# Two-layer hybrid encoder trunk: in the attention loop ScalarE copies every turned probability block two steps behind, and a finished pair's output one step earlier

## The reference, cut to what matters

```python
def block_attention(q, k, v, scale, diag_mask, cum=None):
    for q0 in range(0, S, Q_BLOCK):                # 4 blocks of 128 queries
        q1 = q0 + Q_BLOCK
        s = einsum('bhqd,bhkd->bhqk', q[:, :, q0:q1], k[:, :, :q1]) * scale
        if cum is not None:                        # second attention (FoX)
            s = s + cum[:, :, q0:q1, None] - cum[:, :, None, :q1]
        ...                                        # causal mask
        p = softmax(s, axis=-1)
        outs.append(einsum('bhqk,bhkd->bhqd', p, v[:, :, :q1]))
...
o_a = block_attention(qa, ka, va, mla_scale, chunk_mask) @ w_bo_a
o_b = block_attention(qf, kf, vf, fox_scale, frame_mask, cum) @ w_bo_b
```

## Time and profile before

| | |
|---|---|
| median of 3 runs | 1770.97 us |
| profiled execution | 1771.1 us, its span 1769.3 us, granted TensorE clock 0.996 |
| TensorE busy | 1731.1 us (98%) |
| VectorE busy | 1092.0 us (62%) |
| ScalarE busy | 681.6 us (39%) |
| GpSimd busy | 206.6 us (12%) |

### The profile page before, as it was taken

How to read it: one execution, slowest core, us unless ns; L and a number is a source line. 1 busy time by engine, 2 the same in 40 slices (tenths; PEclk the granted TensorE clock), 3 DMA queues, 4 the chain that set the end, 5 groups by cost and what they waited for, 6 DMA issues and landing times.

```text
span 1769.3 us, 21975 instructions
## 1 busy us (share of the span) xinstructions
PE 1731.1 (98%) x7813; PEld 1375.2 (78%) x7813; DVE 1092.0 (62%) x1647; ACT 681.6 (39%) x1125; POOL 206.6 (12%) x145
## 2 busy tenths in 40 slices
PE   5999999999999999999999999999999999999998
PEld 4777777777888888888877777777778888888886
DVE  7688888757545555543348888867665555555222
ACT  4445544434343233322235555552433422233222
POOL 3621100010020000001125200000100200000010
PEclk9999999999999999999999999999999999999999
DMA  4432211323333333333333312114233333333231
GB/s 124 106 75 75 57 52 42 85 82 95 101 100 94 99 99 95 95 91 95 95 86 70 102 54 60 48 36 113 78 89 113 95 97 98 101 96 92 87 97 69
DMA packets 308468, 152.19 MB, mean 86 GB/s; under 512 B 30436, under 2 KB 307166, under 8 KB 308396
## 3 DMA queue, kind: packets, MB, share of 16 engines
q1 hardware_dynamic: 308096, 151.05, 30.4%
q10 hardware_dynamic: 300, 0.19, 0.0%
HBM read 149.09 MB, written 2.10 MB: 85 GB/s over the span
## 4 chain that ended last, share of the span: by engine, by line
PE 87%; DVE 8%; ACT 3%; issue 2%; DMA 0%; SPq 0%; ACTq 0%; DVEq 0%
PE bank L1293 65%; PE bank L1370 12%; PE bank L1351 4%; PE bank L1403 2%; PE bank L1382 2%; DVE w_lo L912 2%; ACT w_hi L622 1%; DVE h_lo L941 1%; DVE c_acc L972 0%; DMA x_rows<-in_x 0%; DVE tmp L933 0%; PE bank L1318 0%; PE bank L1511 0%; DVE c_raw L1122 0%; DVE rstd_kv L946 0%
## 5 line engine op out<-in xcount | busy, mean ns | idle before, releaser
L622 ACT CAST w_hi<-raw 128x1024 fp32r<-128x1024 f32 (+4 forms) x330 | 301.3, 916 | 733.4 <-PE bank L1293 732.2
L912 DVE TENSOR_TENSOR w_lo<-raw,w_hi 128x1024 fp32r<-128x1024 f32 (+4 forms) x330 | 355.6, 1080 | 239.1 <-ACT w_hi L622 237.8
L1293 PE MATMUL bank<-h_hi,w_hi 128*128 128x512 f32 (+1 forms) x1200 | 474.8, 396 | 10.4 <-DVE w_lo L912 5.4
L1293 PE MATMUL bank<-h_hi,w_lo 128*128 128x512 f32 (+1 forms) x1200 | 468.1, 390 | 0.0
L1293 PE MATMUL bank<-h_lo,w_hi 128*128 128x512 f32 (+1 forms) x1200 | 468.0, 390 | 0.0
L1293 PEld LDWEIGHTS bank<-h_hi,w_hi 128*128 128x128 f32 (+1 forms) x1200 | 225.1, 188 | 69.4 <-issue 12.2
L1293 PEld LDWEIGHTS bank<-h_lo,w_hi 128*128 128x128 f32 (+1 forms) x1200 | 225.2, 188 | 48.9 <-issue 2.5
L1293 PEld LDWEIGHTS bank<-h_hi,w_lo 128*128 128x128 f32 (+1 forms) x1200 | 225.1, 188 | 48.4
L933 DVE TENSOR_TENSOR tmp<-bank,rstd_x 128x512 f32<-128x512 f32 x140 | 96.6, 690 | 267.7 <-PE bank L1293 259.2
L972 DVE SCALAR_TENSOR_TENSOR c_acc<-u_pad,dwk_l,c_acc 128x512 f32<-128x512 f32 x240 | 178.6, 765 | 1.1
L511 POOL TENSOR_TENSOR x_acc<-x_acc,x_sq 128x512 f32<-128x512 f32 x39 | 66.8, 1713 | 881.9 <-ACT x_sq L632 549.2
(11 more groups left out here) (207 smaller groups left out, 2149.0 us busy)
## 6 DMA issues: line engine op xcount, KB each, us to landing
raw<-in_w_in SPq DMA_DIRECT2D x96, 512.0 KB, 3.7
raw<-in_w_ffn_gate SPq DMA_DIRECT2D x44, 512.0 KB, 3.7
raw<-in_w_ffn_up SPq DMA_DIRECT2D x44, 512.0 KB, 3.7
raw<-in_w_ffn_down SPq DMA_DIRECT2D x32, 512.0 KB, 3.7
raw<-in_w_out SPq DMA_DIRECT2D x16, 512.0 KB, 3.8
raw<-in_w_ffn_down SPq DMA_DIRECT2D x16, 384.0 KB, 3.3
raw<-in_w_bo_a SPq DMA_DIRECT2D x16, 256.0 KB, 2.7
raw<-in_w_bo_b SPq DMA_DIRECT2D x16, 256.0 KB, 2.7
```

Of the source, the lines that this page charges most:

```text
L622: last = nc.scalar.copy(to, of)
L912: last = nc.vector.tensor_tensor(to, of, part.bitcast(F32), ALU.subtract)
L1293: ins = nc.tensor.matmul(bank_t[0:rows, :], wt[slot][:, w], x, start=first and k == 0 and p == 0, stop=last and k == k_tiles - 1 and p == 2)
```

## The change

In ScalarE's list for the attention loop, the copy of a transposed block now stands two steps behind its step without exception: block s = 0 is copied in step s = 2, and `pair_out` of the pair before follows it there. Nothing is added or removed, and no other engine's list is touched. One line less is in the file, so what stood from line 672 on now stands one line higher (912 becomes 911).

```diff
                                          accum_out=row_sum[:, s % 4:s % 4 + 1]).then_inc(exp_done, 1)
-                    if s == 3 and pair:
-                        turn(g - 3)
+                    if g >= 2:
+                        turn(g - 2)
+                    if s == 2 and pair:
                         pair_out(pair - 1)
-                    if g >= 2 and (s != 2 or not pair):
-                        turn(g - 2)
                     if g - 2 in FEED_END:
                         split(QKV + FEED_END.index(g - 2) + 2)
                         evac.add()
```

## The result

The changed kernel takes 1781.9 us, the median of 4 runs (1780.75 to 1782.91), against 1771.03 us for the kernel before on the same chip (4 runs, 1770.85 to 1771.8). The ratio is 1.0062 with a 95% interval of 1.0048 to 1.0077: 10.9 us slower. The forecast was 1779.4 us, 8.4 us slower than its own base. The profiled execution took 1782.45 us, its span is 1780.6 us (before 1769.3).

A forecast was written before the change was run, and what follows sets the result against it. TensorE, busy 98%, was taken as the bound. The profiled 1771.1 us + 8.04 us of four waits + 0.4 us beside GpSimd gave 1779.5 us, 1779.4 us for the median; own range 1778 to 1781, wider range 1776 to 1784 us.

The forecast's parts named there:

- Where the kernel is bound: TensorE, busy 98% of the span, sets the time; ScalarE's 11.8 us of copy waits in the first attention loop cost nothing.
- The win of 0 us: Earlier copy and `pair_out` release nothing TensorE waits for; gain bounded by 0 and 0.6 us, taken as 0.
- The path through the cast: Pairs 2 and 5: late `w_hi` cast delays `w_lo` by 3.81 and 3.93 us, then taps, maximum, scaling, TensorE's transposes.
- Size of the four waits: TensorE waits 2.12 us at step 19 and 1.90 us at step 43, in both layers: 8.04 us.
- GpSimd beside `w_lo`: Pair 5: late `w_lo` meets GpSimd's `ob_lo`; bounds 0 to 0.53 us, taken as 0.2 us, 0.4 us in two layers.
- The other five pairs: Pairs 1, 3, 4, 6, 7: late exponential stays hidden, cost nothing; 0.6 us in all if pairs 1 and 4 doubled.
- What is late next: After step 19's wait: step 20's scaling, the late `w_lo` and its `raw` buffer are late, but none reaches TensorE.
- The rule weighed: VectorE's queue is strict first-in first-out; otherwise step 19's scaling would cost TensorE at most about 0.1 us.
- The clock falls in the waits: Rival: all four new TensorE waits bring a clock fall of 2.2 us each, 8.8 us added, 1788.3 us; chance 0.07.
- The granted clock stays where it was: Expected sign in the changed kernel's profile: no change of the granted clock.
- the prediction's own test: Wrong if the four waits are missing, time does not grow by their sum, or transposes wait in the other five pairs.
- The idle 1.83 us near the start: Evidence weighed for the clock rival: after this TensorE idle, at 16.95, no slow matmuls are seen.

The follow-up runs named there:

- experiment 1: Changed kernel, but in pairs 2 and 5 ScalarE casts `w_hi` ahead of the copy and `pair_out`, as before the change: 1771.04 us, ratio 1.0.
- Experiment 2: Kernel before, with only the `w_hi` cast of pairs 2 and 5 put behind `pair_out` in step s = 3: 1781.62 us, ratio 1.0057.
- Experiment 3: Changed kernel, but VectorE makes `w_lo` of pairs 2 and 5 one step later, behind the scaling of steps 19 and 43: 1773.12 us, ratio 1.0012.
- 5 to 7: Changed kernel with VectorE taps at steps 19 and 43 changed: one less 1777.82 us, two less 1776.19 us, one more 1785.33 us.
- change again: Changed kernel run and profiled once more, unedited: 1781.76 us, ratio 1.0059.
- experiment 4: Kernel before, with the change made in pair 2 of each layer alone: 1776.46 us, ratio 1.0032.

## Why the prediction was right, and where its size was off

- **Where the kernel is bound** was right. ScalarE's stall grew by 20 us in the first layer's loop. In experiment 1 it is 18 us longer than before, and the time is that of the kernel before. The win of 0 us was right too: experiment 1 has the earlier copy and `pair_out` and is at 1.0.
- **The path through the cast** was right in each link: copy, `pair_out`, cast, `w_lo` 3.7 us late, two taps, maximum, scaling. Experiment 2 makes it alone, 1 takes it away, 3 cuts it at `w_lo`, and 5 to 7 lengthen and shorten it by 0.66 us per tap.
- **Size of the four waits**: forecast 2 x (2.12 + 1.90), in fact 7.94 us. In pair 2 the wait is 1.93 us instead of 2.12. I measured from the weight load at 191.81, but its matmul starts 0.22 us later (192.03 before the change); behind the wait load and matmul both start at 193.81. The lead of the load is eaten by the wait. In pair 5 the same 0.2 us were offset by the next point. TensorE's matmul at step 19 before the change (its load is in the earlier trace rows):

```profile
192.03 0.60 PE L1382 MATMUL bank<-ident,p_b 128*128 128x128 f32 x4
```

- **GpSimd beside `w_lo`** was right in kind, 0.2 us forecast in both layers. The two rows in pair 5 of layer 0, changed kernel:

```profile
260.09 1.27 POOL L517 TENSOR_TENSOR ob_lo<-o_raw,ob_hi 128x512 fp32r<-128x512 f32 x1 [21.68 <-ACT ob_hi L660]
...
260.99 1.46 DVE L911 TENSOR_TENSOR w_lo<-raw,w_hi 128x1024 fp32r<-128x1024 f32 x1 [4.05 <-ACT w_hi L622]
```

  `w_lo` takes 1.46 instead of 1.22 us, 0.24 us more. In layer 1 it is the same:

```profile
1131.29 1.46 DVE L911 TENSOR_TENSOR w_lo<-raw,w_hi 128x1024 fp32r<-128x1024 f32 x1 [3.85 <-ACT w_hi L622]
```

  With the stretch and without the lead of the load, the forecast 1.90 us becomes 1.90 + 0.24 - 0.22 = 1.92 us. The wait in layer 1 is 1.94 us. In layer 0 it is 2.13 us, and the other 0.2 us lie in ScalarE's list of pair 5, where the first copy of `pair_out` starts 0.37 us after the copy of the block:

```profile
258.57 0.27 ACT L652 COPY p_t<-bank 128x128 f32<-128x128 f32 x1 [4.94 <-PE bank L1402]
258.94 0.59 ACT L659 COPY o_raw<-bank 128x512 f32<-128x512 f32 x1
```

  In layer 1 it is 0.16 us (1129.07 and 1129.23), as at this place before the change (256.74 and 256.90). What holds it up isn't shown. Waits and GpSimd together: 7.94 us, forecast 8.44.
- **The other five pairs** were right: no transpose waits there. VectorE waits 1.3 us at most for a late exponential, but where a cast follows it then waits less for that: in pair 1 of layer 0 1.31 us for the exponential and 0.53 instead of 1.25 us for the cast. `w_lo` starts at 169.45 (forecast: about 169.7), the scaling of step 12 ends at 172.07, and TensorE's load is at 172.65.
- **What is late next** was right for the changed kernel: nothing behind the four waits. Experiment 3 showed how thin that was: 1 us more for VectorE's taps ahead of step 22 came with 1.1 us of waits of TensorE.
- **The rule weighed**: the trace bears out the order of the list. VectorE idled 3.47 and 4.05 us with ready taps behind `w_lo` (pairs 2 and 5 of layer 0), and in experiment 3, with `w_lo` behind the scaling, the wait at step 19 shrank to 0.22 us.
- **The step that was mis-sized: the clock.** "The clock falls in the waits" was priced as none or all four, at 2.2 us each and a chance of 0.07. It happens to single waits. Of the 14 waits of 1.9 to 2.1 us in four profiled executions (change, change again, experiments 2 and 4) 8 were followed by half clock, 1.65 to 1.72 us each. In the profiled execution the two falls, 3.36 us, less the 0.50 us that the waits were smaller than forecast, are 2.9 of the 2.95 us between the sum (1779.5 us) and 1782.45 us. "The granted clock stays where it was" was therefore wrong. The mean of 0.996 hides it, because 7 us at half clock weigh little among 1780 and because the record of this trace misses the slow start.

  By the prediction's own test ("if they are there and the time does not grow by their sum") it failed here: the waits sum to 7.9 us, and the time grew by 10.9. The result lies outside the forecast's own range of 1778 to 1781 us. That it lies inside 1776 to 1784 us is in part luck, since the room there was meant for small stalls in the other pairs, which didn't come, and the falls filled it.

  My reasons were two. The idle 1.83 us near the start seemed to show that such a gap is free, and a dense stream around the waits seemed to protect. But the gap near the start can't show a fall at all. The transposes on both sides of it, in the kernel before:

```profile
11.44 3.67 PE L1442 MATMUL bank<-ident,x_rows 128*128 128x128 f32 x16 [1.65 <-DMA x_rows<-in_x]
16.95 1.85 PE L1442 MATMUL bank<-ident,x_rows 128*128 128x128 f32 x12 [1.83 <-DVE x_t L1059]
```

  Ahead of the gap they start 0.21 us apart, twice the 0.11 us of a transpose in the attention loop, so TensorE was still slow, with no full clock to fall from; behind the gap many are 0.11 us apart. And the stream around the four waits is as dense as anywhere, and the clock fell in it.

Not settled: what decides whether one wait of some 2 us brings a fall. The wait, the work around it and the kernel are the same in the two profiles of the change, so the instruction lists alone don't decide it.

## What to carry to other kernels

In an in-order list, ask of an instruction that will wait not only what it wins but what ready work stands behind it, and follow that work to the bound engine: here 1 us of cast behind a free stall became 2 us of TensorE idle, four times. Before paying for a stall removed, check that it is on the engine that sets the time. And price a new gap in a full TensorE stream at its length plus a possible stretch at half clock, with a spread, instead of as one number.

## What the runs showed of the hardware that was not expected

- After a wait of about 2 us in a stream that is otherwise 98% busy the granted clock fell from 2.4 to 1.2 GHz in 8 of 14 cases, and each fall cost 1.65 to 1.72 us. After 2.6 to 2.8 us it fell in 2 of 4, after 0.6 to 1.5 us in none of 8. The same wait brings a fall or doesn't from one execution to the next. Two falls more or less would make the 3.4 us of spread of the changed kernel's single executions (1780.75 to 1784.13 us), against 0.95 us before; falls themselves are seen only in the profiled executions.
- Of an overlapping GpSimd subtraction and a VectorE tap, the one that starts second is stretched by nearly the whole overlap: two taps from 1.41 to 2.40 us, or GpSimd's operation from 1.28 to 1.86 us. A shift of under 1 us turns which engine pays, and with starts 0.03 us apart it went both ways (experiment 4). In these runs only VectorE's share reached TensorE.
- The mean clock of a profile can miss falls. The changed kernel's trace reads 1.00 for its first 35 us, where matmuls start 0.43 us apart, and its mean of 0.996 equals that of the kernel before. Matched matmul starts showed the falls.
- A weight load's lead of 0.22 us over its matmul is absorbed by a wait: the cost is the wait measured at the matmul, not at the load.
